# Joints of a decoder layer: load order, statistics, attention steps and splits moved

## What is computed

```python
def layer(x, mem, ...):                      # x: 576 tokens x 1024
    mk, mv = split(rmsnorm(mem, g_mem) @ w_mem_kv)   # 256 memory tokens
    h = rmsnorm(x, g_attn)
    zq, zk, zv, zu, zs, zm, zg = split(h @ w_in)     # one input projection
    o_da = diff_attention(zq, zk, zv, caches, rel_bias)
    o_sg = spatial_gate(zu, zs)
    o_mx = cross_attention(zm, mk, mv)
    merged = sum(sigmoid(gate_b) * (o_b @ w_branch_b) for the three branches)
    x = x + merged @ w_out
    a, b = split(rmsnorm(x, g_ffn) @ w_up)           # 1024 -> 2 x 2816
    x = x + (silu(a) * b) @ w_down                   # 2816 -> 1024
    return rmsnorm(x, g_final)
```

## Time and profile before

| | |
|---|---|
| median of three runs | 1336.87 us (1333.18 to 1337.77) |
| the profiled execution | 1337.81 us, span 1335.9 us |
| mean granted clock of TensorE | 0.990 of full speed |
| PE busy | 1307.6 us, 98% of the span |
| DVE busy | 726.6 us, 54% |
| ACT busy | 546.5 us, 41% |
| POOL busy | 127.2 us, 10% |
| DMA | 179.16 MB, mean 134 GB/s |

### The profile page before, as it was taken

One profiled execution on the slowest core, in us unless ns is written; L12 is line 12 of the kernel. 1 busy time (PEld: TensorE's weight loads), 2 busy tenths in 40 slices (PEclk: granted clock), 3 DMA queues, 4 the chain that ended last, 5 costly groups with the idle time before them and its releaser, 6 DMA issues.

```text
span 1335.9 us, 25775 instructions
## 1 busy us (share of the span) xinstructions
PE 1307.6 (98%) x9986; PEld 1237.1 (93%) x9986; DVE 726.6 (54%) x1271; ACT 546.5 (41%) x1062; POOL 127.2 (10%) x157
## 2 busy tenths in 40 slices
PE   8899999999999999999999999998999999999997
PEld 8889999999888888988988889997999999999997
DVE  6656785333566522322344333567888888863333
ACT  5443653113567722212322343255555555552220
POOL 3677000000010100000000000001000000000001
PEclk9999999999999999999999999998999999999998
DMA  6545223524122297857597122331222222122221
GB/s 233 167 151 189 96 95 112 160 93 148 58 90 75 90 294 240 268 191 254 198 332 289 42 64 81 115 128 63 96 94 93 93 90 94 60 89 93 81 94 71
DMA packets 82092, 179.16 MB, mean 134 GB/s; under 512 B 5869, under 2 KB 40941, under 8 KB 80982
## 3 DMA queue, kind: packets, MB, share of 16 engines
q1 hardware_dynamic: 77750, 158.31, 34.7%
q10 hardware_dynamic: 2496, 12.58, 2.7%
q0 software_dynamic: 1760, 7.08, 1.6%
HBM read 166.13 MB, written 14.18 MB: 135 GB/s over the span
## 4 chain that ended last, share of the span: by engine, by line
PE 62%; issue 31%; DVE 3%; POOL 2%; ACT 1%; DMA 1%; POOLq 0%; SPq 0%; ACTq 0%; DVEq 0%
PE acc L2012 42%; PE acc L2187 7%; PE ps L2267 2%; PE ps L2248 2%; PE ps L2324 1%; PE ps L2301 1%; PE ps L2432 1%; POOL ssum L1859 1%; PE ps L2448 1%; PE ps L2258 1%; PE ps L2399 1%; PE ps L2039 1%; PE ps L2209 1%; PE ps L2381 1%; DVE w_lo L1242 0%
## 5 line engine op out<-in xcount | busy, mean ns | idle before, releaser
L1242 DVE TENSOR_TENSOR w_lo<-w_raw,w_hi 128x1024 fp32r<-128x1024 f32 x128 | 160.9, 1257 | 298.5 <-ACT w_hi L733 298.0
L2012 PE MATMUL acc<-h_hi,w_hi 128*128 128x288 f32 x896 | 208.0, 314 | 2.5 <-POOL h_lo L1839 2.4
L733 ACT ACTIVATE w_hi<-w_raw 128x1024 fp32r<-128x1024 f32 x128 | 135.2, 1056 | 168.2 <-PE acc L2514 74.9
L2012 PE MATMUL acc<-h_lo,w_hi 128*128 128x288 f32 x896 | 193.0, 297 | 0.0
L2012 PE MATMUL acc<-h_hi,w_lo 128*128 128x288 f32 x896 | 192.8, 297 | 0.0
L2012 PEld LDWEIGHTS acc<-h_hi,w_hi 128*128 128x128 f32 x896 | 142.8, 190 | 13.8 <-issue 9.1
L2012 PEld LDWEIGHTS acc<-h_hi,w_lo 128*128 128x128 f32 x896 | 144.3, 189 | 0.0
L2012 PEld LDWEIGHTS acc<-h_lo,w_hi 128*128 128x128 f32 x896 | 144.2, 189 | 0.0
L2187 PE MATMUL acc<-xs_lo,w_hi 128*128 128x288 f32 x352 | 104.9, 298 | 0.0
L2187 PE MATMUL acc<-xs_hi,w_lo 128*128 128x288 f32 x352 | 104.8, 298 | 0.0
L2187 PE MATMUL acc<-xs_hi,w_hi 128*128 128x288 f32 x352 | 104.4, 297 | 0.0
(11 more groups left out here) (388 smaller groups left out, 2929.0 us busy)
## 6 DMA issues: line engine op xcount, KB each, us to landing
w_raw<-w_stream SPq DMA_DIRECT2D x158, 512.0 KB, 3.6
v_pg<-cache_v SPq DMA_DIRECT2D x32, 512.0 KB, 4.7
w_raw_b<-w_stream SPq DMA_DIRECT2D x22, 512.0 KB, 4.2
k_even<-cache_k SPq DMA_DIRECT2D x16, 512.0 KB, 7.1
k_odd<-cache_k SPq DMA_DIRECT2D x16, 512.0 KB, 6.7
km_pg<-mem_k ACTq DMA_DIRECT2D x6, 1024.0 KB, 6.4
vm_pg<-mem_v ACTq DMA_DIRECT2D x6, 1024.0 KB, 6.8
x_sb<-xT SPq DMA_DIRECT2D x8, 576.0 KB, 5.9
```

The costliest lines, as they stand in the source:

```text
L733: nc.scalar.activation(w_hi[:, u, :], w_raw[:, u, :], ACT.Copy).then_inc(w_hi_done, 1)
L1242: nc.vector.tensor_tensor(w_lo[:, u, :], w_raw[:, u, :], w_hi[:, u, :].bitcast(F32), ALU.subtract)\
L2012: last = nc.tensor.matmul(acc[a][:, c, 0:n], w[:, u, k * P:(k + 1) * P], x[:, k0 + k, c * n:(c + 1) * n], start=start and k == 0 and t == ...
```

## The change

Five edits; none changes what is computed.

1. SP issues x pairs 2 and 3 each behind one more weight panel: panel 2, x pair 2, panel 3, x pair 3, instead of all x pairs first.
2. `norm_stats(1)` stands behind panel `mv` 0 instead of behind the last `mk` panel, on PE; on DVE it stands behind the low split that comes with panel `mv` 0.
3. Every prompt step is issued two k tiles later.
4. The pair of unit QK is loaded two `w_out` panels earlier. Its sums 3 and 4 get places of their own (`cp` and `rms_b`, in place of `w_sum`), so that POOL need not wait for the last panels, and the copy of product 0 into `cp` waits for the lows. ACT's first high parts and DVE's first low parts move one panel earlier. PE's `norm_stats(2)` stands behind product 3 and `norm_bcast(2)` behind product 5.
5. The splits of the second `down` panel stand ahead of tile 7 of `g_hi` and `g_lo` instead of at the end of the last unit.

```diff
--- before.py
+++ after.py
@@ -298,6 +298,8 @@
             return pair_at(j, i, w_lo, w_lo_q, w_lo_b)
 
         def pair_s(j, i):
+            if isinstance(i, int) and i == QK and j >= 3:
+                return cp[:, :, :].rearrange("p a n -> p (a n)")[:, 0:KW] if j == 3 else rms_b[:, 0:KW]
             return w_sum[:, j - 3, :] if j >= 3 else (w_sum_q if early_unit(i) else w_sum_b)[:, j, :]
 
         def pair_part(j, i, s):
@@ -585,10 +587,13 @@
                 load_w(c, c, 0)
             sp.dma_start(cst[:, :], consts).then_inc(cst_loaded, 16)
             sp.dma_start(b_sel[:, :], bias_select).then_inc(sel_loaded, 16)
-            for c in range(4):
+            for c in range(2):
                 load_x(c, x_loaded[c])
+            for c in range(2):
+                load_w(2 + c, c, 0)
+                load_x(2 + c, x_loaded[2 + c])
             sp.dma_start(pages[:, :], page_table).then_inc(pages_loaded, 16)
-            stream(2, FIRST["s"] + 4, 0)
+            stream(4, FIRST["s"] + 4, 0)
 
             sp.wait_ge(line_ready, 2)
             sp.dma_start(line_d, rel_line[:, :]).then_inc(line_stored, 16)
@@ -702,10 +707,10 @@
                 load_w(FIRST["mx_proj"] + 3 + 2 * c, 1)
                 sp.wait_ge(acc_free[1], FIRST["mx_proj"] // 2 + c + 1)
                 load_x(c, x_loaded[c])
-            stream(FIRST["w_out"] + 2, FIRST["w_out"] + 6)
+            stream(FIRST["w_out"] + 2, FIRST["w_out"] + 4)
             sp.wait_ge(o_lo_done, 4 * KT)
             load_pair(QK, 1, STREAM_AT["up"])
-            stream(FIRST["w_out"] + 6, FIRST["down"])
+            stream(FIRST["w_out"] + 4, FIRST["down"])
             sp.wait_ge(w_lo_done, FIRST["down"])
             load_pair(QK + 1, 0, STREAM_AT["up"])
             with sp.Fori(QK // 2 + 1, UNITS // 2) as i:
@@ -853,6 +858,8 @@
                     out = square[:, 0:HT]
                 else:
                     out = gate[:, c * HT:(c + 1) * HT] if early_unit(i) else cp[:, c, :]
+                if c == 0 and isinstance(i, int) and i == QK:
+                    act.wait_ge(pair_lo_done, NJ * QK + 4)
                 nc.scalar.activation(out, pair_bank(j, i, s), ACT.Copy, scale=scale).then_inc(pair_copied, 1)
 
             for n in range(KT):
@@ -1149,7 +1156,7 @@
                     nc.scalar.activation(xs_hi[:, k, 5:7, :], xs_raw[:, k, 5:7, :], ACT.Copy).then_inc(x_hi, 1)
                     nc.scalar.activation(xs_hi[:, k, 2, :], scaled[:, 1, 0:HT], ACT.Copy).then_inc(x_hi, 1)
                     resid_square(n, u, 2, tile)
-                if n == KT - 3:
+                if n == KT - 4:
                     for j in (0, 1, 2):
                         hi_of(j, QK, 1)
                 if n == KT - 2:
@@ -1185,9 +1192,6 @@
                 nc.scalar.activation(gate[:, :], scaled[:, 0, :], ACT.Silu).then_inc(ffn_silu, 1)
                 if not last:
                     hi_of(6, i + 1, 1 - s)
-                else:
-                    act.wait_ge(pair_mm, NJ * i + 7)
-                    split_hi(FIRST["down"] + 1, 1)
 
             def g_hi_tile(k):
                 act.wait_ge(pair_out, 4 * (QK + k + 1))
@@ -1205,6 +1209,8 @@
                 g_hi_tile(k)
             up_unit(UNITS - 1, 0, last=True)
             for k in range(G_LATE, FT):
+                if k == G_LATE + 4:
+                    split_hi(FIRST["down"] + 1, 1)
                 if k == 13:
                     act.wait_ge(mm_done, FIRST["down"] + 1)
                     split_hi(FIRST["down"] + 2, 0)
@@ -1348,13 +1354,13 @@
                     nc.vector.tensor_copy(col(M_RS, w=2), col(N_RS, w=2)).then_inc(stat_pow, 1)
                 if n == 4:
                     lam_columns()
-                if n == 7:
-                    norm_stats(1, T)
             for n in range(KT):
                 p, u = FIRST["mv"] + n, n % 2
                 wait(dve, turned, n - 1)
                 early_out(p, u, mv_turn[:, u, :])
                 split_lo(p + 2, u)
+                if n == 0:
+                    norm_stats(1, T)
                 if n == 2:
                     dve.wait_ge(rms_ready, 2)
                 for k in X_TILES[n]:
@@ -1721,9 +1727,10 @@
                     nc.vector.tensor_tensor(xs_lo[:, k, 2, :], b2[:, 0:HT], xs_hi[:, k, 2, :].bitcast(F32), ALU.subtract)\
                         .then_inc(x_lo, 1)
                 add_square(n, u, 2)
-                if n >= KT - 3:
-                    if n < KT - 1:
-                        first_lows(QK, n - (KT - 3))
+                if n == KT - 4:
+                    first_lows(QK, 0)
+                if n == KT - 2:
+                    first_lows(QK, 1)
             first_lows(QK, 2)
             norm_stats(2, T)
 
@@ -1768,9 +1775,7 @@
                 nc.vector.tensor_tensor(g_tile[:, HT:T], gate[:, HT:T], b2, ALU.mult)
                 dve.wait_ge(pair_mm, NJ * i + 7)
                 nc.vector.tensor_tensor(g_tile[:, 0:HT], gate[:, 0:HT], pair_bank(6, i, s), ALU.mult).then_inc(pair_out, 1)
-                if last:
-                    split_lo(FIRST["down"] + 1, 1)
-                else:
+                if not last:
                     lo_of(6, n, t)
 
             def g_lo_tile(k):
@@ -1788,6 +1793,8 @@
                 g_lo_tile(k)
             up_unit(UNITS - 1, 0, last=True)
             for k in range(G_LATE, FT):
+                if k == G_LATE + 4:
+                    split_lo(FIRST["down"] + 1, 1)
                 if k == 13:
                     split_lo(FIRST["down"] + 2, 0)
                 if k == 20:
@@ -1899,7 +1906,7 @@
                 for j, a, b, op in ((1, a21, a22, ALU.add), (2, pair_s(1, i), a11, ALU.subtract),
                                     (3, a12, pair_s(2, i), ALU.subtract), (4, a11, a21, ALU.subtract)):
                     wait(pool, pair_sum, 4 * i + j - 1)
-                    if j == 3:
+                    if j == 3 and panels_end:
                         pool.wait_ge(mm_done, panels_end - 1)
                     nc.gpsimd.tensor_tensor(pair_s(j, i), a, b, op).then_inc(pair_sum, 1)
 
@@ -1987,7 +1994,7 @@
                 nc.gpsimd.tensor_copy(q_mb[:, b % 2, :, 0:TS], zmT[:, :, SEQ + b * TS:SEQ + (b + 1) * TS]).then_inc(m_q, 1)
 
             pool.wait_ge(mm_done, FIRST["w_out"])
-            first_sums(QK, FIRST["down"])
+            first_sums(QK, 0)
 
             norm_pow(2, T)
             norm_pow(3, T)
@@ -2286,7 +2293,7 @@
                 panel(FIRST["u"] + 6 + u, u, h_hi, h_lo)
             for c in range(KT):
                 slot_free("da_gate", c // 2, c % 2)
-                panel(FIRST["da_gate"] + c, c % 2, h_hi, h_lo, behind=lambda k: p_step(8 * c + k - 2))
+                panel(FIRST["da_gate"] + c, c % 2, h_hi, h_lo, behind=lambda k: p_step(8 * c + k - 4))
 
             def s_score(b):
 
@@ -2356,7 +2363,7 @@
 
             def zone_step(c, k):
                 if c < 2:
-                    p_step(8 * (KT + c) + k - 2)
+                    p_step(8 * (KT + c) + k - 4)
                 if k == KT // 2 - 1:
                     sample_step(2 * c)
                 elif k == KT - 1:
@@ -2492,9 +2499,9 @@
                 if j < 2:
                     pe.wait_ge(acc_free[j], FIRST["down"] // 2)
                 product(j, QK, 1, first=True)
-                if j == 1:
+                if j == 3:
                     norm_stats(2, T)
-                if j == 3:
+                if j == 5:
                     norm_bcast(2, T)
             for j in range(NJ):
                 product(j, QK + 1, 0)
```

## The result

The changed kernel takes 1341.85 us (median of 9 runs, 1339.88 to 1344.61) against 1336.87 before. The medians differ by 5.0 us; the ratio on record is 1.0044, with an interval of 1.0033 to 1.0055, which is 5.9 us slower, at least 4.4. The time lies inside the range of the forecast, 1333.5 to 1344, and 1.9 us above the forecast time. But the interval of the ratio leaves out 1: the result is on the side of the rivals "slower", where the forecast said no measurable change.

The account below looks back on a forecast made before the run. TensorE, busy 98% of the span, bounds the kernel; only idle stretches and slow clock behind them can move. Terms -3.4 + 0.9 + 1.3 + 5.0 - 0.7 = +3.1 us on the median give 1340.0 us, range 1333.5 to 1344.

Parts of the forecast that it names:

- the rivals "slower": Whole kernel: rival cases forecasting more than 0.3% slower, at 1342.0 to 1343.4 us; chance of slower 0.33.
- Part 1: Third memory-key panel: weights issued ahead of x tiles land sooner, removing a 1.78 us wait and slow clock; -3.4 us.
- the 1.66 us for the slow stretch: Third memory-key panel: time lost in a 4.37 us window at 0.62 clock, counted as saved within the -3.4.
- Part 2: Input's statistics: the stall moves to the broadcast, 2.9 us, instead of vanishing; +0.9 us (bounds -0.25 and +1.2).
- Part 3: Prompt's steps: first wait goes (-1.2), but late weight splits stall seven panel boundaries 0.36 us each; +1.3 us.
- Part 4: Up joint: statistics behind product 3 uncover a 4.74 us chain ahead of product 4; +5.0 us (bounds -0.6 and +7.6).
- The forecast's rival: POOL's sums lock DVE for their whole length, 1.32 to 1.52 us each; sum +5.1, 1342.0 us; chance 0.08.
- Part 5: Down joint: without two splits in front, k tile 3 starts sooner; -0.7 us (bounds -1.5 and -0.3).
- the low clock in the up joint: Up joint: rival with half clock from product 2 to product 6, +7.6; sum +5.7, 1342.6 us; chance 0.22.
- the lock's 1342.0: Time forecast by the rival that POOL's sums lock DVE for their whole length; chance 0.08.

Follow-up runs that it names:

- e6: Kernel before with only the input's statistics moved behind the first memory-value panel on PE (on DVE the same); 1336.9 us, ratio 1.0006.
- e12: Kernel before with only weight panels 2 and 3 issued ahead of x pairs 2 and 3; 1335.61 us, ratio 0.9993.
- e3: Changed kernel with the prompt's steps one k tile later than before instead of two; 1341.78 us, ratio 1.0033.
- e9: Changed kernel with unread filling matmuls at the up joint: 9 ahead of product 1, 6 ahead of product 2, 19 behind the statistics; 1338.69 us, ratio 1.0022.
- e4: Changed kernel with all up-joint edits undone and the prompt's steps one k tile later than before instead of two; 1333.54 us, ratio 0.9985.
- e5: Changed kernel with unread filling matmuls at the up joint: 19 ahead of product 1, 14 ahead of product 2, 38 behind the statistics; 1343.42 us, ratio 1.0048.
- e2: Changed kernel with the early pair load, POOL sums and first high and low parts undone, statistics still behind product 3; 1340.7 us, ratio 1.0034.
- e1: Changed kernel with the up joint's statistics back behind product 1 and their broadcast behind product 3; 1335.7 us, ratio 1.0002.
- e8: Changed kernel with ACT's copy of product 2 of unit QK ahead of the split of the next unit's first sum; 1341.05 us, ratio 1.0030.
- e10: Kernel before with earlier memory weights, down-joint edit, prompt's steps one k tile later, fillings of 9 (input's statistics), 9 and 11 (up joint); 1332.28 us, ratio 0.9965.
- e7: Kernel before with earlier memory weights, down-joint edit, prompt's steps one k tile later, 19 fillings each ahead of product 1 and up-joint statistics; 1333.85 us, ratio 0.9977.
- e11: As e10, with the up joint's early sums added and its statistics still behind product 1; 1332.14 us, ratio 0.9966.

## Why the prediction was right, and where it was not

- **Part 1** was right in the trace (-3.50 for -3.4, landing at 14.58 for 14.6) and too large as a term of the time: alone it brings 0.9 us, with an interval that ends at 2.4. The step that failed is the 1.66 us for the slow stretch, booked as if every execution had it: e6 has the same wait with the clock at 1.00 behind it. That the traces agree with the forecast is no test of this, as both rest on the same trace of before. What is left without it is some 1.9 us (-1.8 by the forecast's own bound), which the interval of e12 holds. In e12's trace 1.1 us more went at 727.8. How often the clock falls there in executions of before stays open.
- **Part 2** was right in its mechanism (a stall of 2.81 for 2.9). The stretch came to -0.4 in the trace of after, with the clock up (the bound there was -0.25), and, from the end of the last `mk` panel, to +0.7, +0.8, +1.3, +1.6 and +2.5 in e3, e9, e6, e4 and e5 with the clock down, three of them above the upper bound of 1.2. In e2 the clock fell too, but the stretch came to -0.4, as its clock was at 1.00 from 75 to 90 us, where before has 0.89. The value taken, +0.9, lies between.
- **Part 3**: 0.33 us at each of seven boundaries for the forecast 0.36; +0.94 for +1.3.
- **Part 4** was the part that decides and was read rightly down to its times. On the clock of before (2.60 added) product 4 starts at 936.9, between the forecast's 934.9 and 938.7, product 6 ends at 944.9 for 944.2, and L1696 starts at 920.0 for 919.7. e1 shows that the place of the statistics is the loss, e8 that the chain runs through ACT's queue, and e9 with e10 that the chain is most of it and the clock some 1 us. In the forecast's sum the uncovered chain at full clock costs only 1.6 us (940.8 for 939.2), since the 939.2 of before already holds low clock; the rest of its +5.0 is the choice of a point near half clock.
- **POOL and DVE.** The four slowed DVE operations took 3.7 us more than in the earlier trace rows and their unslowed neighbours, for the forecast 3.3. Three of them end 0.31 to 0.32 us after the sum beside them and the double-length one 0.62, whatever part of the sum they had waited: that is the exclusive lock of the Trainium skill, "SBUF — State Buffer", section "Who interferes with whom", and the trace agrees with it. The forecast's rival misread the rule: by these rows a lock costs what is left of the sum when DVE comes, not the sum's length (5.5 us for the four sums of before; the forecast says 5.3). The delay was won back before the end of the output panels.
- **Part 5**: -0.75 for -0.7.
- **The whole.** By its terms the trace comes to +2.1 from panel 1 to the first `down` panel, for +3.1; the runs say +5.9, with 4.4 as the least. The direction was right and the size was about half. The term mis-sized against the times is part 1; against the one trace it is part 2, too high, and part 4, too low by 0.6. With the times where a part was timed alone (part 1 -0.9, part 2 +0.8, the place of the statistics +5.6) and the trace for the others (+0.9 and -0.7), the sum is +5.7; the first three are uncertain by 1.5 to 2 us each. Of the rivals, the low clock in the up joint came nearest: three slow stretches were there, but the clock was back at full when product 6 ran. That the lock's 1342.0 is nearer still to 1341.85 is chance; its mechanism is the one that the rows above refute.

## What to carry to other kernels

Before moving an instruction behind others, follow what waits for its result on every engine's queue: here the statistics blocked DVE, DVE's sum blocked ACT, and ACT's copy blocked the product after next, so two products of cover were worth more than the wait that they were to hide. A stall ahead of TensorE costs its length and, where the clock falls, the slow stretch behind it, up to 1.9 us at the three stalls of this joint. Filling stalls with matmuls of the right total length made e9 2.9 us faster than the changed kernel; for the joint of e10 the traces show 0.8 to 2.7 us less than for the same order without fillings. A fall of the clock that is seen in one trace is booked as a chance, not as a term, until other traces of the same place show it.

## What was not expected of the hardware

All nine kernels with part 2 have nearly the same idle stretch, 2.7 to 2.9 us ahead of the input's broadcast, with the same instructions of TensorE before it. The clock behind it was 1.00 in three of the traces (the changed kernel, e1 and e8) and 0.58 to 0.73 in six (e2, e3, e4, e5, e6 and e9). From the end of the last `mk` panel to that of the last `mv` panel, the three are 0.2 to 0.3 us shorter than before and the six 1.1 to 2.5 us longer. The third memory-key panel shows the same: 0.62 behind 1.78 us in before, 1.00 behind 1.75 us in e6. A 128x128 float32 matmul written once ran as two, 0.22 us in all. At the up joint the clock was at 1.00 throughout in the four kernels whose fillings left no idle time over 0.75 us there (e5, e7, e10, e11), and at 0.66 in e9 behind 2.10 us of it.
